# Half-block products in twelve up-projection steps, with weight sums made by accumulating transfers

## What is computed

```python
D_MODEL = 1024; SEQ = 512; D_FF = 2816; CONV_W = 3; DEPTH = 2
def conv_ffn(h, w_up, conv_w, conv_b, w_down):
    u = h @ w_up                                   # 1024 -> 2 x 2816
    up = jnp.pad(u, ((0, 0), (CONV_W - 1, 0), (0, 0)))
    u = conv_b + sum(conv_w[j] * up[:, j:j + S] for j in range(CONV_W))
    gate, val = jnp.split(u, 2, axis=-1)
    return (jax.nn.silu(gate) * val) @ w_down
...
x = x + m
x = x + conv_ffn(rms_norm(x, norm_ffn[layer]), ...)
```

## Time and profile before

| | |
|---|---|
| time, median of 3 runs | 1191.7 us (1190.4 to 1191.9) |
| the profiled execution's own time | 1191.57 us |
| its span, first to last instruction | 1189.8 us |
| PE busy | 1174.8 us, 99% of the span, 6874 matmuls |
| DVE, ACT, Pool busy | 73%, 52%, 29% |
| mean granted clock of PE | 0.998 |
| up projections | about 297 to 534 us and 834 to 1071 us |
| down projections | about 541 to 648 us and 1078 to 1185 us |
| first attention, second mixer and attention | about 174 to 252 us, 648 to 793 us |

### The profile page before, as it was taken

One profiled execution on the slowest core, in us unless ns is written; L12 is line 12 of the kernel. 1 busy time (PEld: TensorE's weight loads), 2 busy tenths in 40 slices (PEclk: granted clock), 3 DMA queues, 4 the chain that ended last, 5 costly groups with the idle time before them and its releaser, 6 DMA issues.

```text
span 1189.8 us, 18961 instructions
## 1 busy us (share of the span) xinstructions
PE 1174.8 (99%) x6874; PEld 999.6 (84%) x6874; DVE 862.7 (73%) x1502; ACT 617.0 (52%) x1033; POOL 348.5 (29%) x429
## 2 busy tenths in 40 slices
PE   9999999999999999999999999999999999999998
PEld 7768886778888888888999887988888888888998
DVE  6588968945766566579897898855766666579986
ACT  6554337855434333345565789945534334335563
POOL 0633547830042522211000366730042421211000
PEclk9999999999999999999999999999999999999999
DMA  7555352253398785436554110053387574326553
GB/s 281 182 187 199 142 202 65 73 142 106 106 238 238 199 217 184 175 109 211 186 160 138 62 37 2 1 125 107 106 192 179 156 172 130 106 71 208 176 173 127
DMA packets 51555, 174.54 MB, mean 147 GB/s; under 512 B 4720, under 2 KB 6128, under 8 KB 41504
## 3 DMA queue, kind: packets, MB, share of 16 engines
q1 hardware_dynamic: 36352, 127.51, 31.3%
q0 software_dynamic: 15136, 46.14, 16.3%
HBM read 171.50 MB, written 52.47 MB: 188 GB/s over the span
## 4 chain that ended last, share of the span: by engine, by line
PE 93%; DVE 3%; ACT 2%; issue 1%; POOL 0%; DVEq 0%; ACTq 0%; POOLq 0%
PE ps L2554 28%; PE ps L2556 27%; PE ps L2555 27%; PE ps L2269 3%; PE ps L2253 3%; PE ps L2069 1%; PE ps L2520 1%; PE ps L2110 1%; PE ps L2237 1%; PE ps L2140 1%; ACT probs L977 1%; DVE w_lo L1705 1%; DVE xT L1725 0%; PE ps L2121 0%; ACT w_hi L1148 0%
## 5 line engine op out<-in xcount | busy, mean ns | idle before, releaser
L2554 PE MATMUL ps<-h_hi,w_hi 128*128 128x512 f32 x704 | 274.4, 390 | 0.0
L2555 PE MATMUL ps<-h_lo,w_hi 128*128 128x512 f32 x704 | 273.9, 389 | 0.0
L2556 PE MATMUL ps<-h_hi,w_lo 128*128 128x512 f32 x704 | 273.9, 389 | 0.0
L1394 DVE TENSOR_TENSOR w_lo<-raw,w_hi 128x2048 fp32r<-128x2048 f32 (+1 forms) x62 | 123.0, 1984 | 118.3 <-ACT w_hi L887 118.3
L1216 ACT ACTIVATE cv<-u_in,vec 128x512 f32<-128x512 f32 x88 | 71.2, 816 | 180.4 <-DVE u_in L1835 178.3
L887 ACT ACTIVATE w_hi<-raw 128x2048 fp32r<-128x2048 f32 (+1 forms) x72 | 121.8, 1692 | 69.1 <-PE ps L2556 69.1
L2554 PEld LDWEIGHTS ps<-h_hi,w_hi 128*128 128x128 f32 x704 | 132.2, 188 | 27.6 <-issue 0.7
L2556 PEld LDWEIGHTS ps<-h_hi,w_lo 128*128 128x128 f32 x704 | 132.2, 188 | 27.6
L2555 PEld LDWEIGHTS ps<-h_lo,w_hi 128*128 128x128 f32 x704 | 132.2, 188 | 27.3
L762 POOL TENSOR_TENSOR v<-act 128x256 f32<-128x256 f32 x16 | 43.3, 2707 | 345.2 <-DVE act L1872 345.2
L2554 PE MATMUL ps<-a_hi,w_hi 128*128 128x256 f32 (+1 forms) x440 | 138.9, 316 | 2.2 <-DVE a_lo L1709 2.2
(11 more groups left out here) (276 smaller groups left out, 2421.6 us busy)
## 6 DMA issues: line engine op xcount, KB each, us to landing
raw<-in_f_up SPq DMA_DIRECT2D x44, 1024.0 KB, 5.0
w_sums<-in_f_w_down POOLq DMA_DIRECT2D x22, 1024.0 KB, 8.7
w_sums<-in_f_w_down POOLq DMA_DIRECT2D x44, 512.0 KB, 9.0
raw<-w_sums SPq DMA_DIRECT2D x44, 512.0 KB, 4.2
raw<-in_a_in_wide SPq DMA_DIRECT2D x12, 1024.0 KB, 6.1
raw<-in_f_w_down SPq DMA_DIRECT2D x22, 512.0 KB, 3.9
raw<-in_f_w_down SPq DMA_DIRECT2D x22, 256.0 KB, 4.0
bias_tiles<-bias_rows SPq DMA_DIRECT2D x1, 4096.0 KB, 27.0
```

The costliest lines, as they stand in the source:

```text
L1394: dve.tensor_tensor(w_lo[:, s, 0:n], raw[:, s, 0:n], w_hi[:, s, 0:n].bitcast(F32), ALU.subtract)\
L2554: pe.matmul(dst, s_hi, m_hi, start=start, stop=False)
L2555: pe.matmul(dst, s_hi, m_lo, start=False, stop=False)
L2556: return pe.matmul(dst, s_lo, m_hi, start=False, stop=stop)
```

## The change

Steps 5 to 8 of layer 0 and 1 to 8 of layer 1 (`SEVENS`) are made as seven products of half blocks: features and channels (gate, value) are halved on the weights' side, features and tokens on the other. Each product has two parts of 128 channels, 4 feature tiles, 3 matmuls of 256 tokens. The weights of all steps but step 0 come in units of 128 x 1024 floats (512 KB) in a ring of four (`raw4`, `hi4`, `lo4`), seven for a seven step, four for a plain one. Three of the seven are plain blocks, four are sums: Pool copies blocks into `w_two` and `w_more` in DRAM (`copy_up`), and accumulating transfers add to them (`two_up` 1 MB, `three_up` and `four_up` 512 KB each). Per layer four sums of the normed features are made (`gained_features` on ACT, `sums_of_features` on DVE) and split (`sum_hi`, `sum_lo`). ACT takes partial results out of PSUM (`keep`), DVE adds and scales them (`first_row`, `second_row_sum`, `second_row`); of a seven step, the second row, the taps and the gating are done in the following step.

Pool's transfers are placed anew. Layer 0: `copy_up` among `pool_lo` in place of nine `copy_weights`, `two_up` behind the first attention, `three_up`, `four_up` in step 0, the eleven `copy_weights` a quarter step apart in steps 1 to 3, `sum_weights` two a quarter in step 4, then one a product. Layer 1: sixteen `copy_up` (1 MB each) at every second count of `r_used[1]` in layer 0's down stage, four `two_up` at its last count, four more between the two scalings of `b_w_ukv`, `three_up` behind the tails of keys, `four_up` and `copy_weights` among the second attention's `normed`, `sum_weights` every second product of steps 1 to 7. `gate_sums` of pairs 3 to 10 wait for the last seven step (one more step after it has begun). In the second `onto_residual`, `gained_features(1)` stands ahead of `root_of_mean` and `sum_hi(1, 0)` behind it on ACT; on DVE the two halves of `sums_of_features(1)` stand before and behind `token_rstd`, and `sum_lo(1, 0)` behind them. The loops are written out.

```diff
+SEVENS = ((5, 6, 7, 8), (1, 2, 3, 4, 5, 6, 7, 8))
...
+UP_UNITS = [[(i, j) for i in range(1, UP_STEPS) for j in range(7 if i in SEVENS[l] else 4)] for l in range(2)]
...
+                for m, (i, j) in enumerate(UP_UNITS[l]):
+                    r = m % 4
+                    sp.wait_ge(w_lo_done, U_UP[l] + (1 + m // 2 if m < 4 else m - 1))
+                    if i in SEVENS[l]:
+                        z = SEVENS[l].index(i)
+                        if z == 0 and j in (1, 2, 5):
+                            sp.wait_ge(up_sums, sums_made(l, {1: 3, 2: 4, 5: 5}[j]))
+                        src = (f_up[l, i, 0, :, 0:D], w_two[l][z][:, D:2 * D], w_more[l][z][:, 0:D], f_up[l, i, 0, :, D:2 * D],
+                               w_two[l][z][:, 0:D], w_more[l][z][:, D:2 * D], f_up[l, i, 1, :, D:2 * D])[j]
+                    else:
+                        src = f_up[l, i, j // 2, :, (j % 2) * D:(j % 2 + 1) * D]
+                    sp.dma_start(raw4[:, r, :], src).then_inc(f_raw[r], 16)
...
+            def copy_up(l, z, h):
+                src = f_up[l, SEVENS[l][z]]
+                if h:
+                    pool.dma_start(w_more[l][z], src[0], max_dma_last_dim=8192).then_inc(up_sums, 16)
+                else:
+                    pool.dma_start(w_two[l][z].rearrange("p (a n) -> p a n", a=2), src[:, :, 0:D].rearrange("s p n -> p s n"))\
+                        .then_inc(up_sums, 16)
...
+            def two_up(l, z):
+                if z == 0:
+                    pool.wait_ge(up_sums, sums_made(l, 2))
+                pool.dma_start(w_two[l][z], f_up[l, SEVENS[l][z], 1], accum_op=ALU.add, max_dma_last_dim=8192)\
+                    .then_inc(up_sums, 16)
+            def three_up(l, z):
+                if z == 0:
+                    pool.wait_ge(up_sums, sums_made(l, 3))
+                pool.dma_start(w_more[l][z][:, 0:D], w_two[l][z][:, D:2 * D], accum_op=ALU.add).then_inc(up_sums, 16)
...
+            def sums_of_first():
+                for z in range(len(SEVENS[0])):
+                    two_up(0, z)
+                behind(0, 0, 1)
+                for z in range(len(SEVENS[0])):
+                    three_up(0, z)
+                behind(0, 0, 3)
+                for z in range(len(SEVENS[0])):
+                    four_up(0, z)
+                for i in range(1, 4):
+                    for j in range(4):
+                        behind(0, i, j)
+                        if 4 * i + j - 4 < G_PAIRS:
+                            copy_weights(0, 4 * i + j - 4)
+                        if j == 1:
+                            gate_sums(0, i - 1)
+                for j in range(4):
+                    behind(0, 4, j)
+                    sum_weights(0, 2 * j)
+                    sum_weights(0, 2 * j + 1)
+                for k in range(8, FT):
+                    behind(0, *UP_UNITS[0][unit_of(0, 5) + k - 8])
+                    sum_weights(0, k)
+                for i in range(3, G_PAIRS):
+                    gate_sums(0, i)
+                for c in range(2 * len(SEVENS[1])):
+                    pool.wait_ge(r_used[1], 2 * c + 1)
+                    copy_up(1, c // 2, c % 2)
+                pool.wait_ge(r_used[1], G_USED)
+                for z in range(4):
+                    two_up(1, z)
...
+            for z in range(4, 8):
+                two_up(1, z)
...
+                    three_up(1, w - 2 * T)
...
+                if u % 2 == 0 and 2 <= u < 18:
+                    four_up(1, u // 2 - 1)
+                elif u % 2 and u >= 3:
+                    copy_weights(1, (u - 3) // 2)
...
+            def unit_hi(l, m):
+                if m >= len(UP_UNITS[l]):
+                    return
+                r = m % 4
+                sc.wait_ge(f_raw[r], unit_landed(l, m))
+                sc.wait_ge(f_done, unit_used(l, m - 4))
+                sc.activation(hi4[:, r, :], raw4[:, r, :], ACT.Copy).then_inc(w_hi_done, 1)
...
+                def keep(i, j):
+                    x, _, v_bank = seven_banks(l, i)
+                    bank, dst = {0: (x, kept[:, 0].rearrange("p (a n) -> p a n", a=2)),
+                                 1: (v_bank, kept[:, 1].rearrange("p (a n) -> p a n", a=2)),
+                                 2: (x, u_in[:, 0:2, 2 + HS:2 + S]), 4: (x, u_in[:, 2:4, 2 + HS:2 + S])}[j]
+                    z = SEVENS[l].index(i)
+                    sc.wait_ge(f_done, DONE_AT[l][i] + j + 1)
+                    if j < 2 and z:
+                        sc.wait_ge(f_in, IN_AT[l][i - 1] + j + 1)
+                    if j >= 2:
+                        sc.wait_ge(f_t0, 2 * FT * l + 4 * (i - 1) + j)
+                    sc.activation(dst, both(ps[:, bank, :]), ACT.Copy).then_inc(f_snap, 1)
...
+                        sc.activation(rbc_minus[:], ps[:, 1, :], ACT.Copy, scale=-1.0).then_inc(rbc_ok, 1)
+                        if l:
+                            for j in (1, 2, 3):
+                                sum_hi(1, j)
...
+            def sums_of_features(l, part):
+                if part == 0:
+                    dve.wait_ge(t_gained, LANDED + KD * l + 4)
+                    dve.tensor_tensor(t_raw[0], x11, x12, ALU.subtract).then_inc(t_summed, 1)
+                    dve.wait_ge(t_gained, LANDED + KD * (l + 1))
+                    dve.wait_ge(t_summed, LANDED + 4 * l + 1)
+                    dve.tensor_tensor(x12, x22, x12, ALU.subtract).then_inc(t_summed, 1)
+                else:
+                    dve.wait_ge(t_summed, LANDED + 4 * l + 2)
+                    dve.scalar_tensor_tensor(x11, x12, -1.0, x11, ALU.mult, ALU.subtract).then_inc(t_summed, 1)
+                    dve.wait_ge(t_summed, LANDED + 4 * l + 3)
+                    dve.scalar_tensor_tensor(x21, x11, -1.0, x21, ALU.mult, ALU.subtract).then_inc(t_summed, 1)
+            def sum_lo(l, j):
+                dve.wait_ge(t_hi_ok, LANDED + 4 * l + j + 1)
+                dve.tensor_tensor(quarters(t_lo[j]), t_raw[j], quarters(t_hi[j]).bitcast(F32), ALU.subtract)\
+                    .then_inc(t_lo_ok, 1)
...
+                def first_row(i, t):
+                    _, y, v_bank = seven_banks(l, i)
+                    if t == 0:
+                        dve.wait_ge(f_done, DONE_AT[l][i] + 4)
+                        dve.wait_ge(f_snap, LANDED + SNAP_AT[l][i] + 1)
+                        dve.wait_ge(f_t0, 2 * FT * l + 4 * (i - 1) + 2)
+                        dve.tensor_tensor(u_in[:, 0:2, 2:2 + HS], both(kept[:, 0]), both(ps[:, y, :]), ALU.add)\
+                            .then_inc(f_in, 1)
+                    else:
+                        dve.wait_ge(f_done, DONE_AT[l][i] + 6)
+                        dve.wait_ge(f_snap, LANDED + SNAP_AT[l][i] + 3)
+                        x = u_in[:, 0:2, 2 + HS:2 + S]
+                        dve.tensor_tensor(x, x, both(ps[:, v_bank, :]), ALU.add).then_inc(f_in, 1)
+                        dve.wait_ge(f_in, IN_AT[l][i] + 3)
+                        x = u_in[:, 0:2, 2:2 + S]
+                        dve.tensor_tensor(x, x, rbc[:].unsqueeze(1).to_broadcast([P, 2, S]), ALU.mult).then_inc(f_in, 1)
+                def second_row_sum(i):
+                    dve.wait_ge(f_snap, LANDED + SNAP_AT[l][i] + 4)
+                    x = u_in[:, 2:4, 2 + HS:2 + S]
+                    dve.tensor_tensor(x, x, both(kept[:, 1]), ALU.add).then_inc(f_in, 1)
+                def second_row(i):
+                    bank = seven_banks(l, i)[0]
+                    minus = [rbc_minus[:, t * HS:(t + 1) * HS].unsqueeze(1).to_broadcast([P, 2, HS]) for t in range(2)]
+                    dve.wait_ge(f_done, DONE_AT[l][i] + 7)
+                    dve.wait_ge(f_t0, 2 * FT * l + 4 * (i - 1) + 4)
+                    dve.tensor_tensor(u_in[:, 2:4, 2:2 + HS], both(ps[:, bank, :]), minus[0], ALU.mult).then_inc(f_in, 1)
+                    dve.wait_ge(f_in, IN_AT[l][i] + 2)
+                    x = u_in[:, 2:4, 2 + HS:2 + S]
+                    dve.tensor_tensor(x, x, minus[1], ALU.mult).then_inc(f_in, 1)
...
+                def plain_step(i):
+                    m = unit_of(l, i) if i else -4
+                    if i - 1 in SEVENS[l]:
+                        second_row(i - 1)
+                        unit_lo(l, m + 3)
+                        taps(i - 1, (0, 1))
+                        taps(i - 1, (2, 3))
+                        gated(i - 1)
+                    scaled(i, 0)
+                    scaled(i, 1)
+                    if i == UP_STEPS - 1:
                         third(l, 0)
                         seven_lo(l, 0, 0)
                         seven_lo(l, 0, 1)
-                    else:
-                        lo(U_UP[l] + 2 * i + 2, SLOT, 0)
+                    elif i:
+                        unit_lo(l, m + 4)
+                        unit_lo(l, m + 5)
                     taps(i, (0, 1))
-                    scaled(i, 2, first)
-                    scaled(i, 3, first)
+                    scaled(i, 2)
+                    scaled(i, 3)
+                    if l and i == 0:
```

(68 more changed lines are left out.)

313 lines of the change are left out of this document (223 added, 90 removed).

## The result

The changed kernel takes 1212.0 us (median of four, 1210.7 to 1212.9), the kernel before beside it 1191.8 us (1190.4 to 1192.6). The ratio is 1.017, 95% interval 1.015 to 1.019: slower, 16 us beyond the forecast and 6 us beyond the end of its range. The profiled execution has a span of 1211.0 us, against 1189.8.

A forecast was written before the change was run, and what follows sets the result against it. TensorE, holding 93% of the chain of waits, was taken as the bound. Terms -21.0 + 4.7 + 8.5 + 3.3 + 8.5 + 0.5 = +4.5 gave 1196 us, range 1184 to 1206.

The forecast's parts named there:

- Part 1: Seven steps: 168 matmuls of 256 columns in 20.0 us replace 96 of 512 in 21.75; gain 21.0 us over twelve steps.
- Parts 3 and 4: First seven step of each layer: PE waits for unit 2's split; gaps of 4.7 us in layer 0, 8.5 in layer 1.
- Part 8: Second mixer's start: layer 1's `two_up` delay `b_w_uq` and `b_w_ukv` loads, engines taking rows in turn; 8.5 us, bounds 0 to 12.
- Part 5: PE's clock: half clock for about 3.3 us behind each of two new holes; 3.3 us lost, bounds 0 and 5.
- Part 7: Layer 0's down stage: layer 1's 16 MB of copies run beside the loads; cost 0 to 1 us.
- Parts 2 and 6: Inside seven steps: DVE busy 18.6 of 20.0 us, half loads in 6 to 6.5 us; both cost 0, part 6 at most 4.
- Part 9: Second attention: Pool's added `four_up` and copies use up the slack before PE's transpose; 0.5 us, bounds 0 and 4.
- The rival of the late loads: Seven steps run at the pace of DVE or of the loads, each late by the excess; 1203 us, chance 0.18.

The follow-up runs named there:

- e6: The changed kernel with e5's placement of Pool's transfers and e1's order on ScalarE and VectorE together; 1189.4 us, ratio 0.998 to the kernel before.
- e1: The changed kernel with ScalarE and VectorE reordered around each layer's first seven step, unit 2's split first; 1203.8 us, ratio 1.009 to the kernel before.
- e10: The changed kernel with layer 1's second four `two_up` issued behind the second scaling of `b_w_ukv` instead of ahead of it; 1210.9 us in one run.
- e9: The changed kernel with layer 1's eight `two_up` as plain copies of the same size and place, the addition left out; 1218.1 us in one run.
- e4: The changed kernel with eight of layer 1's `copy_up` moved from layer 0's down stage into steps 9 and 10, the rest later and thinner; 1207.6 us.
- e11: The kernel of e8 with `gate_sums` of pairs 3 to 8 spaced a quarter step apart and all sixteen layer 1 `copy_up` in layer 0's down stage; 1180.2 us.
- e2: The changed kernel with useless matmuls put where PE waits for unit 2 of each layer's first seven step; 1210.1 us.
- e8: The kernel of e6 with six small edits: `two_up`, `three_up`, `four_up` moved, `keep` earlier, splits reordered at the hand-overs; 1181.1 us, ratio 0.991 to the kernel before.
- e5: The changed kernel with all of Pool's transfers placed anew, order of ScalarE and VectorE unchanged; 1196.1 us, ratio 1.005 to the kernel before.
- e3: The changed kernel with layer 1's `two_up` moved from the second mixer's start to the tails of keys, `three_up`, `four_up` and weight copies later; 1209.0 us.

## Why the prediction was wrong, point by point

- *Part 1, fewer matmuls*: right. From 888.42 to 949.78 us of e6, three steps, PE takes 61.36 us with one hole of 0.94: 20.1 a step, against 20.0 forecast.
- *Parts 3 and 4, the first seven steps*: right to 0.4 us (4.67 and 8.83 us for 4.7 and 8.5), each ended by the split of unit 2, and e1 shows that the order is the cause. (The terms of part 3 add up to 10.3 us, not 10.4, which changes nothing.)
- *Part 8, `two_up` at the mixer*: right in amount (8.6 us for 8.5) and mostly in mechanism. The second load of `b_w_uq` landed 11.6 us after its issue (11.3 forecast), the first of `b_w_ukv` 17.8 (18.4). The hole of 5.55 us is the late transpose that part 8 put at 4, the one of 3.06 is the rest, behind the last scaling, as laid out there, and e10 shows that the four issues ahead of that scaling make it. (The batch's "4 x 5.9 = 22" adds up to 23.6.) That the addition's 5.9 us a MB sets the delay is shown in part: without it (e9) `b_w_ukv` lands 7.8 us sooner and the first hole is 2.02, but the first load of `b_w_uq` isn't sooner at all. Which rule the engines share by isn't settled by that.
- *Part 5, the clock*: **the term that failed most**, 3.3 us for 8.0 (9.7 less the 1.7 of before). Two terms were wrong. I took the 3.3 us of half clock of the earlier trace rows for every hole, where the longer holes here had 3.8 to 5.4; and I counted the fall behind parts 3 and 4 only, though by my own parts 8 must leave one too (2.4), and the down stage left a fourth (2.7).
- *Part 7, the copies in the down stage*: **the place that failed most**, 0 to 1 forecast and put into the sum at 0, 3.9 + 0.4 us of holes measured, and with the 2.7 of clock behind them 7.0. I compared a mean rate with a mean need, but the copies begin late, behind `gate_sums`, and then the first three go out within 4.2 us:

```profile
550.46 0.70 POOL L825 DMA_DIRECT2D w_two<-in_f_up  x1
551.04 0.66 POOL L823 DMA_DIRECT2D w_more<-in_f_up  x1
554.61 0.66 POOL L825 DMA_DIRECT2D w_two<-in_f_up  x1 [2.91 <-PE ps L2953]
```

  The load of `w_sums` that SP issued at 553.2, between the second and the third, landed 13.8 us later, and VectorE waited for it, and PE for VectorE:

```profile
567.11 0.69 DVE L1976 TENSOR_TENSOR raw<-raw 128x512 f32<-128x512 f32 x1 [6.31 <-DMA raw<-w_sums]
```

  e4, with fewer and later copies there, takes the hole away. In e11 all sixteen are in the down stage again, 2.4 counts apart instead of 2, the first three go out in 7.3 us, and the hole doesn't come back, which points to how close they follow one another and not to their number; e11 differs from the change in more, so the two are not shown apart. The order of Pool's queue stood in the code; I did not follow it there.
- *Parts 2 and 6, inside the seven steps*: 0 forecast, 2.4 us measured, within the upper bound of 4. A half load landed in 7.2 (`f_up`) to 8.3 us (`w_more`) in 900 to 960, not 6 to 6.5: my count for layer 1, one sum every second product, should have given 7 x 1.4 + 3.5 x 3.1 = 20.7 us of transfers in 20.0 us, over-full as in layer 0, and I had made that sum for layer 0 only. Behind the first large hole PE is itself late, which hid more of the same: e1 and e2 uncovered it. In 900 to 960 the queues of Pool and SP together held the DMA engines 52.7 + 45.8 = 98.5% of the time. The way from a late load to PE led over `keep`, which the prediction had listed as not on the path: both holes ended with it, and e8, which puts it ahead of the taps, has none over 0.4 us left there.
- *Part 9*: 0.35 us for 0.5.
- *Not in the sum*: 0.7 us at 273 us, where four `two_up` of layer 0 meet the loads of `a_w_out` (part 8's collision at another place, gone in e5), and 1.5 us at 6 and 10 us, which the edits don't explain: no transfer of Pool is issued there before 50 us, and the other changed kernels of this study have 0.3 to 2.0 in that place, the kernel before none. Last, each hole costs about 0.2 us beyond its idle time: from 931.59 to 953.48 PE takes 21.89 us with a hole of 1.60, which leaves 20.29, where the undisturbed step from 973.61 to 993.67 takes 20.06. Ten new holes make some 2.3 us, and twelve steps of 20.06 instead of 20.0 another 0.7, together 3. With the clock's 8.0 that is, to 0.2, the 10.8 us missing from busy time.

The sum of misses: clock 4.7, holes of the down stage 4.3, seven steps 2.4, start and `a_w_out` 2.2, restarts and step length 3: some 16.6 us, about the 16 by which the forecast was short. The rival of the late loads, at 1203, was nearest, and right in kind but not in place.

VectorE's 18.6 of 20 us in part 2 took each operation at its price alone. That held where no `gate_sums` ran: VectorE was busy 18.8 us in 980 to 1000. Beside them it doesn't hold. The Trainium skill, "SBUF — State Buffer", section "SBUF: two separate sides", says that VectorE with two operands in SBUF and a GpSimd operation that reads SBUF lock each other out for a whole instruction. The rows of e8 above agree (a split pair of 3.69 us instead of 2.36). In the change eleven of the 116 splits of L1969 took 1.45 to 1.76 us, all beside `gate_sums`, and none of the holes above came there; the other 105 took 1.21 to 1.25, 33 of them beside a DMA issue of Pool. In the down stages, where splits and `gate_sums` hardly meet, the mean is 1222 ns:

```profile
L1969 DVE TENSOR_TENSOR w_lo<-raw,w_hi 128x1024 fp32r<-128x1024 f32 x116 | 143.6, 1257 | 20.9 <-ACT w_hi L1320 20.8
L1986 DVE TENSOR_TENSOR w_lo<-raw,w_hi 128x1024 fp32r<-128x1024 f32 x66 | 80.7, 1222 | 21.8 <-ACT w_hi L1335 21.8
```

## What to carry to other kernels

Transfers that feed a later stage must be costed per stretch (their time plus that of the loads, against the stretch), and their first issue read from the queue of the engine that issues them: a batch held back by other work comes out in one piece. A hole in PE costs its idle time, about 0.2 us for the restart, and up to 2.7 us of half clock, and every hole of the sum gets that term. Where one stage's kind of step follows another's, look at what the shared engines do between the last operation of the old kind and the first that the new kind waits for; here two such orders were worth 8 us and the placement of transfers 16. Both together (e6) made a change that lost 20 us into one that gains 3, and the small orders and placements of e8 and e11 brought that to 12.

## What the runs showed of the hardware

- Loads of SP that meet four 1 MB transfers of Pool land late: 768 KB in 11.1 and 11.6 us instead of 4.3 beside adding transfers, 11.7 and 9.2 beside plain copies; 512 KB right behind them in 17.8 instead of 5.3, and 10.0 beside plain copies.
- After holes of 3.9 to 8.8 us PE worked 3.8 to 5.4 us at half clock, the least behind the longest hole, where the clock had been down for some 6 us before PE started again.
- After short holes the clock falls in some runs and not in others. All thirteen kernels have a hole of 1.4 to 1.5 us at one and the same place, the start of the second mixer (1.41 at 673.7 in the change): behind it the clock fell in ten, the kernel before among them, and not in the change, e3 and e5. Holes of 1.0 to 1.7 us in e1's seven steps left the clock at 1.00; in step 4 of layer 1 one of 1.80 did so too (e2) and one of 1.85 did not (e4). What tells these apart is not settled here.
- While PE is at half clock others catch up: making it fast again in e2 gained nothing in layer 0.
- A VectorE split of 1.22 us takes up to 1.76 beside Pool's additions in the change, and 1.22 beside its DMA issues.
